# Both parts of x streamed as 512 columns in the feed-forward gate and up projections, and results rounded after the next job's first split, on one Trainium2 core

## What is computed

```
m = (jax.nn.sigmoid(z[..., o_gs:o_ga]) * (y_ssm @ w_proj_ssm[l])
     + jax.nn.sigmoid(z[..., o_ga:]) * (y_attn @ w_proj_attn[l]))
x = x + m @ w_out[l]
h = rms_norm(x, norm2_w[l], RMS_EPS)
x = x + (jax.nn.silu(h @ w_ffn_gate[l]) * (h @ w_ffn_up[l])) @ w_ffn_down[l]
```

## Time and profile before

| | |
|---|---|
| median of three runs | 2527.08 us |
| the profiled execution, its own time | 2526.77 us |
| its span, first to last instruction | 2525.0 us |
| TensorE busy | 2460.2 us, 97% |
| VectorE, ScalarE, GpSimd busy | 1475.3, 1129.0 and 186.0 us |
| granted TensorE clock, mean | 0.993 of full speed |

### The profile page before, as it was taken

The page is one execution under the profiler, slowest core; times in us unless marked ns, Lnnn a source line. Parts: engine busy times, 40 slices in busy tenths (PEclk is TensorE's granted clock), DMA queues, the critical chain, the costliest instruction groups (busy, mean ns, idle before and its releaser), DMA issues.

```text
span 2525.0 us, 45210 instructions
## 1 busy us (share of the span) xinstructions
PE 2460.2 (97%) x19625; PEld 2249.2 (89%) x19625; DVE 1475.3 (58%) x1814; ACT 1129.0 (45%) x1562; POOL 186.0 (7%) x198
## 2 busy tenths in 40 slices
PE   7999999999999999999999999999999999999997
PEld 7777888999889999999988899899888898999885
DVE  4899955565444545445444445745645567456555
ACT  5565555544444444444443344423544535234542
POOL 4000000001000000000000001310100051201000
PEclk9999999999999999999999999999999999999998
DMA  8444444454545555565555576423537664235465
GB/s 235 133 150 147 149 142 132 128 182 166 200 149 182 179 184 181 186 184 184 185 191 191 192 221 176 118 86 116 163 107 239 173 216 135 86 102 151 127 199 167
DMA packets 259414, 412.43 MB, mean 163 GB/s; under 512 B 53072, under 2 KB 74064, under 8 KB 258704
## 3 DMA queue, kind: packets, MB, share of 16 engines
q1 hardware_dynamic: 254496, 395.57, 50.7%
q0 software_dynamic: 4400, 13.89, 2.0%
q10 hardware_dynamic: 320, 0.08, 0.0%
HBM read 403.17 MB, written 6.30 MB: 162 GB/s over the span
## 4 chain that ended last, share of the span: by engine, by line
PE 90%; DVE 6%; ACT 2%; issue 1%; POOL 0%; DMA 0%; ACTq 0%; SPq 0%; DVEq 0%
PE bank L561 88%; DVE wp_lo L1069 2%; ACT wp_hi L1722 1%; PE bank L768 0%; DMA xt<-x 0%; DVE r_a L1548 0%; DVE rsd L1194 0%; DVE nsd L1461 0%; DVE r_kb L1550 0%; ACT L1722 0%; PE bank L662 0%; DVE xr L1715 0%; DVE xr L1713 0%; DVE sqr L1204 0%; POOL sgsA L2170 0%
## 5 line engine op out<-in xcount | busy, mean ns | idle before, releaser
L1069 DVE TENSOR_TENSOR wp_lo<-raw,wp_hi 128x1024 fp32r<-128x1024 f32 x740 | 921.0, 1251 | 893.9 <-ACT wp_hi L1722 893.5
L1722 ACT ACTIVATE wp_hi<-raw 128x1024 fp32r<-128x1024 f32 x740 | 782.5, 1060 | 1123.5 <-PE bank L561 1096.0
L561 PE MATMUL bank<-XX_hi,wp_hi 128*128 128x256 f32 x3840 | 1113.0, 290 | 10.8 <-DVE wp_lo L1069 9.7
L561 PE MATMUL bank<-XX_lo,wp_hi 128*128 128x256 f32 x3840 | 1087.5, 283 | 0.0
L561 PE MATMUL bank<-XX_hi,wp_lo 128*128 128x256 f32 x3840 | 1087.2, 283 | 0.0
L561 PEld LDWEIGHTS bank<-XX_hi,wp_hi 128*128 128x128 f32 x3840 | 736.6, 192 | 29.5 <-DVE wp_lo L1069 12.6
L561 PEld LDWEIGHTS bank<-XX_lo,wp_hi 128*128 128x128 f32 x3840 | 737.1, 192 | 2.2 <-issue 1.9
L561 PEld LDWEIGHTS bank<-XX_hi,wp_lo 128*128 128x128 f32 x3840 | 736.5, 192 | 0.0
L561 PE MATMUL bank<-wp_hi,FF_hi 128*128 128x512 f32 x352 | 137.3, 390 | 0.0
L561 PE MATMUL bank<-wp_hi,FF_lo 128*128 128x512 f32 x352 | 137.1, 389 | 0.0
L561 PE MATMUL bank<-wp_lo,FF_hi 128*128 128x512 f32 x352 | 137.1, 389 | 0.0
(11 more groups left out here) (476 smaller groups left out, 2774.7 us busy)
## 6 DMA issues: line engine op xcount, KB each, us to landing
raw<-w_in SPq DMA_DIRECT2D x304, 512.0 KB, 3.8
raw<-w_out SPq DMA_DIRECT2D x96, 512.0 KB, 4.1
raw<-w_ffn_gate SPq DMA_DIRECT2D x88, 512.0 KB, 3.8
raw<-w_ffn_up SPq DMA_DIRECT2D x88, 512.0 KB, 4.3
raw<-w_ffn_down SPq DMA_DIRECT2D x88, 512.0 KB, 3.6
raw<-w_proj_attn SPq DMA_DIRECT2D x16, 512.0 KB, 4.0
raw<-w_proj_ssm SPq DMA_DIRECT2D x16, 512.0 KB, 3.6
raw<-w_glu SPq DMA_DIRECT2D x8, 512.0 KB, 3.4
```

The source lines that it names most:

```text
L561: return e.matmul(o, lhsT, rhs, start=start, stop=stop, skip_group_check=True)
L1069: return tt(d, src, hi, SUB)
L1722: return e.activation(o, x, func, bias=bias, scale=scale)
```

## The change

1. `Pair` holds hi and lo in one buffer; `tiles(k)` gives both as a 128 x 2 x 256 view. For the 22 gate and up jobs (`wide`) a step has, per output tile, one matmul of w.hi with that view (512 columns, a whole bank: first half hi·hi, second half hi·lo) and one of w.lo with x.hi (256 columns, added to the first half). Each job takes four banks, 0 to 3 or 4 to 7.
2. The halves of a bank are added by VectorE with a `tensor_reduce` over a view that puts the halves innermost: four per job, 512 values in and 256 out per partition, into `gt` for gate and into `sqr` for up. ScalarE's SiLU now reads `gt` in SBUF and waits for these; up's multiply reads `gt` and `sqr`.
3. A function `rest` holds the rounding and subtraction of the results of `ps` and `fu`. Both engines call it after the split in the next job's first piece, not in `evac`.
4. VectorE's function `rest` for the mixer's angles is renamed; it does the same.

```
-        j.banks = (0, 1) if i % 2 == 0 else (2, 3)
+        j.banks = tuple(range(4 * (i % 2), 4 * (i % 2) + 4)) if j.wide else (0, 1) if i % 2 == 0 else (2, 3)
...
+    sides = lambda a: a.rearrange("p (h t) -> p t h", h=2)
...
+            elif j.wide:
+                for m in range(4):
+                    d, c = B[j.banks[m]], (512 * i + 128 * m, 512 * i + 128 * m + 128)
+                    mm(d, w.hi(*c), XX.tiles(k), first, False)
+                    last = mm(d[:, 0:256], w.lo(*c), XX.tile(k)[0], False, end)
...
 VectorE:
-                if n == "ps":
-                    e.wait_ge(*MSA("h", c))
-                    w = slice(1024 * c, 1024 * c + 1024)
-                    lo(MM.l[:, w], flat(sgs(c)), MM.hi_f(w.start, w.stop)).then_inc(MSV.made("l", c), 1)
...
+            elif n[:2] == "fg":
+                c = int(j.name[2:])
+                for m in range(4):
+                    if c > 1 and m % 2 == 0:
+                        e.wait_ge(*FSV("l", 2 * c - 4 + m // 2))
+                    w = slice(256 * (m % 2), 256 * (m % 2) + 256)
+                    e.tensor_reduce(gt[2 * (c % 2) + m // 2][:, w], sides(b[m]), AXX, ADD).then_inc(s_evV, 1)
             elif n[:2] == "fu":
...
-                e.wait_ge(s_evA, NA[f"fg{c}"])
+                for m in range(4):
+                    if c and m % 2 == 0:
+                        e.wait_ge(*FUV("m", 2 * c - 2 + m // 2))
+                    w = slice(256 * (m % 2), 256 * (m % 2) + 256)
+                    e.tensor_reduce(sqr[m // 2][:, w], sides(b[m]), AXX, ADD).then_inc(s_evV, 1)
                 for i in range(2):
-                    tt(g[i], g[i], b[i], MUL).then_inc(s_evV, 1)
-                for i in range(2):
-                    m = 2 * c + i
-                    e.wait_ge(*FSA("h", m))
-                    lo(FF.lo(512 * m, 512 * m + 512), g[i], FF.hi_f(512 * m, 512 * m + 512)).then_inc(FSV.made("l", m), 1)
+                    e.wait_ge(s_evV, j.freed[2 * i + 1][1])
+                    e.wait_ge(*FGA("s", 2 * c + i))
+                    tt(g[i], g[i], sqr[i], MUL).then_inc(FUV.made("m", 2 * c + i), 1)
...
+        def rest(name):
+            if name[:2] == "ps":
+                c = int(name[2:])
+                e.wait_ge(*MSA("h", c))
+                w = slice(1024 * c, 1024 * c + 1024)
+                lo(MM.l[:, w], flat(sgs(c)), MM.hi_f(w.start, w.stop)).then_inc(MSV.made("l", c), 1)
+            elif name[:2] == "fu":
+                c = int(name[2:])
+                for i in range(2):
+                    m = 2 * c + i
+                    e.wait_ge(*FSA("h", m))
+                    lo(FF.lo(512 * m, 512 * m + 512), gt[2 * (c % 2) + i], FF.hi_f(512 * m, 512 * m + 512)).then_inc(FSV.made("l", m), 1)
...
                         split(p + 3)
+                    if PIECE[p - 1][3]:
+                        rest(PIECE[p - 1][0].name)
                     if t + 1 == ENDS[j.name]:
                         evac(j)
...
 ScalarE (its rest and main change in the same way):
                 for i in range(2):
-                    if c > 1:
-                        e.wait_ge(*FSV("l", 2 * c - 4 + i))
-                    act(gt[2 * (c % 2) + i], b[i], ACT.Silu).then_inc(s_evA, 1)
...
+                    e.wait_ge(s_evV, j.freed[2 * i + 1][1])
+                    act(gt[2 * (c % 2) + i], gt[2 * (c % 2) + i], ACT.Silu).then_inc(FGA.made("s", 2 * c + i), 1)
```

More of the change, by code:

```diff
@@ L86, in __init__ @@
         self.name, self.W, self.pieces, self.KT = name, W, pieces, KT
-        self.home, self.tokens, self.first = home, tokens, first
+        self.home, self.tokens, self.first, self.wide = home, tokens, first, len(home) == 4
 class Pace:
@@ L178, in __init__ @@
         def __init__(self, name, n):
-            self.h, self.l = place(name + "_hi", n, F32R), place(name + "_lo", n, F32R)
+            self.both = v3(place(name + "_hl", 2 * n, F32R)[:, :], 2)
+            self.h, self.l = self.both[:, 0, :], self.both[:, 1, :]
         def hi(self, a, b):
@@ L194, in tile, with tiles @@
             return self.hi(256 * k, 256 * k + 256), self.lo(256 * k, 256 * k + 256)
+        def tiles(self, k):
+            return self.both[:, :, 256 * k:256 * k + 256]
     cst = alloc("cst", NCONST)
@@ L614, in step @@
             if first:
-                bank(j.banks[0], *freed(j.name, 0))
-                bank(j.banks[1], *freed(j.name, 1))
+                for m, b in enumerate(j.banks):
+                    bank(b, *freed(j.name, m))
             operand(j, k)
@@ L1078, in evac @@
             b = [B[x] for x in j.banks]
-            if n not in ("gs", "ga", "glu", "rg", "cg", "mg0", "mg1") and n[:2] != "fg":
+            if n not in ("gs", "ga", "glu", "rg", "cg", "mg0", "mg1"):
                 e.wait_ge(*over(j.name))
@@ L1348, in turn, with rest_of_angle @@
             last.then_inc(TU.made("fr", t), 1)
-        def rest(t):
+        def rest_of_angle(t):
             u = sets[t % 2]
@@ L1367, in _ @@
         turn(0)
-        rest(0)
+        rest_of_angle(0)
         for t in range(16):
@@ L1388, in _ @@
             if t < 15:
-                rest(t + 1)
+                rest_of_angle(t + 1)
             main(at.share(4.3))
@@ L1842, in evac, with rest @@
                     hi(MXc.hi(512 * i, 512 * i + 512), pair(cy, i)).then_inc(BXA.made("h", 2 * int(l) + i), 1)
+        def rest(name):
+            if name[:2] == "ps":
+                c = int(name[2:])
+                e.wait_ge(*GSP("a", 2 * c + 1))
+                hi(MM.hi(1024 * c, 1024 * c + 1024), flat(sgs(c))).then_inc(MSA.made("h", c), 1)
+            elif name[:2] == "fu":
+                c = int(name[2:])
+                for i in range(2):
+                    m = 2 * c + i
+                    e.wait_ge(*FUV("m", m))
+                    hi(FF.hi(512 * m, 512 * m + 512), gt[2 * (c % 2) + i]).then_inc(FSA.made("h", m), 1)
         def main(steps):
```

18 lines of the change are left out of this document (4 added, 14 removed).

## The result

The changed kernel takes 2511.45 us in the median of six runs (2508.51 to 2518.45), the kernel before 2527.18 (2525.52 to 2528.19); the ratio is 0.9944, 95% interval 0.9931 to 0.9957. It is faster, inside the range forecast and 0.75 us from the forecast. The six times lie in two places, though: 2508.5, 2508.7, 2510.8 and 2512.1, and 2518.1 and 2518.5. The kernel before keeps within 3 us. The profiled execution is the slowest of the six, with a span of 2516.7 us.

A forecast was written before the change was run, and what follows sets the result against it. TensorE, busy 97% of the span, was taken as the bound. Wide matmuls 18.8 + ps jobs 3.2 - fg2's end 2.7 - clock 2.9 = 16.4 us saved, from 2526.77 to 2510.4, median 2510.7; range 2506 to 2521.

The forecast's parts named there:

- The rate of the wide matmuls: Gate/up: a group takes 346.7 ns in place of 360.0, saving 13.3 ns in each of 1408 groups, 18.8 us.
- the sign named in the prediction: Gate/up trace: 512- and 256-column matmuls start 227 and 120 ns apart in turn, pieces 2.77 us apart.
- The 2.5 ns of the Trainium skill: Gate/up, opposing estimate: a removed instruction saves 2.5 ns, 3.5 us in all; result about 2526.
- The ps jobs: Ends of four ps jobs: rounding behind the next split gets back 0.80 us each, 3.2 us.
- The evacuations: End of fg: reduces 0.60 us apart, ScalarE's split 5.32 after its previous split's start (T), 0.38 to spare, cost 0.
- "Cost 0": End of fu: VectorE done at 7.11 us against 8.06 needed, 0.95 to spare; roundings follow the split, nothing lost.
- The end of fg2: Four reduces ahead of the angles delay everything by 2.40 us; TensorE late by 3.52, not 0.80: cost 2.72, idle 3.36.
- The clock: Behind fg2's idle time the granted clock drops, costing 2.9 us, bounds 0 and 3.2; no-drop rival: 2507.8, chance 0.28.
- the two that had a drop: Kernel before: idle times of 3.76 and 3.74 us, followed by granted clocks of 0.56 and 0.60.
- The sum: Whole kernel: 16.4 us saved, from 2526.77 to 2510.4, as a median of runs 2510.7; chance 0.40.
- dearer reduces: Rival, evacuations: outputs are paid for, 0.87 us per reduce, 9.5 us together, 2520.2; chance 0.11.

The follow-up runs named there:

- part 3 alone: Kernel before, with only rounding and subtraction of ps and fu results moved behind the next job's first split, no wide matmuls: 2524.04 us, ratio 0.9986.
- the wide-only kernel, grouped: Changed kernel with rounding and subtraction put back into the evacuation, and each step's four 512-column matmuls ahead of its four of 256: 2526.45 us.
- the grouped changed kernel: Changed kernel with each step's four 512-column matmuls ahead of its four of 256, nothing else changed: 2513.23 us.

## Why the prediction was right, and what it missed

**The rate of the wide matmuls** was right as a size and wrong as a constant. The 346.7 ns a group came from two streams of equal matmuls; at the quick pace it is 346.7. The sum held and its terms did not: the sign named in the prediction was starts of 227 and 120 ns in turn, and they are 231 or 232 and 115 or 116. A removed instruction saved 13 ns. The 2.5 ns of the Trainium skill, "TensorE: Matmul & The Clock Gate", section "Back-to-back issue gap", is for an isolated gap and isn't what it saves in this stream, as the trace of the kernel before had said. What the step took for granted, that a sequence of 512 and 256 columns has the sum of their rates, holds only in one of two paces. In the other a group takes 353.3, and 17 of 22 jobs then save 6.7 ns a group in place of 13.3: 7 us less of the 18.8.

**The ps jobs**: 3.2 forecast; by part 3 alone 3.0 between medians and 3.7 between profiles. The prediction took the loss to be 0.80 at each of the four; at ps3 it was 0.4 more.

**The evacuations**: reduces 0.60 apart as assumed, the split at T + 5.29 for 5.32, slack 0.32 for 0.38. At the end of fu ScalarE's split starts at T + 2.8, a piece later, and TensorE isn't late. "Cost 0" held.

**The end of fg2**: 2.40 us by four reduces forecast; from T to TensorE 9.18 before and 11.55 after, 2.37. The idle time printed is 3.32 for 3.36.

**The clock** fell in all three profiles of the changed kernel, at 2.9 us forecast and 2.8 measured. That my gap was nearer to the two that had a drop was a weak reason. Seven profiles have 3.2 to 3.3 us idle behind fg2; in six the clock fell, one of them at 3.23 us too (the wide-only kernel, grouped), and in the grouped changed kernel it didn't at 3.23. And the wait of 1.73 us in the attention stage was followed by a drop in two of the twelve profiles, and not in that of the kernel before.

**The sum** holds at the quick pace. Gate/up was to gain 18.8 - 2.7 - 2.9 = 13.2 us, and in the two profiles at that pace it is 13.0 and 12.9 us shorter; with 3.7 at ps the change gains 16.6 or 16.7, for 16.4 forecast. That is 2510.1, where half of the runs are (2508.5 to 2512.3); the others are 7 us and more above. My forecast describes the first set. That the median of six came within 0.75 us of it is luck: four of the six were quick, and the median of all 16 is 4 us above. The slower set lies inside the range only because that reached to 2521 for dearer reduces, which there were not. What remains open: why alternating 512 and 256 has two paces, and whether the 3 us of the attention stage's clock come with the change. Two of nine profiles of kernels with wide matmuls have that drop and none of three without, behind the same 1.73 us of idle time; that is too few to tell.

## What to carry to other kernels

Work out for each end of a job when the next operand is ready against when it is wanted, on each engine in its own order; here a rounding in front of a split cost some 10 us at the fu jobs, half of what 1408 saved matmuls gave, and 3.7 at the ps jobs. When an edit puts work into a place that is already late, move that place's other work first: spreading nine small instructions took away a wait, a drop of the clock and a restart that could cost the pace. And when the runs of a kernel fall into two sets, compare the distance of starts in a profile of each before looking for a cause in one.

## What the runs showed of the hardware

A TensorE stream that alternates 512 and 256 columns has two paces, 346.7 and 353.3 ns a group, drawn at a restart, after 0.3 us of delay as well as after 3 us, and kept as long as the engine isn't kept waiting; most of the difference, 5 ns, is in the 512-column matmul. Uniform streams ran at one pace each (120.0 and 226.7 ns). Four of one length followed by four of the other ran at 350.8 a group throughout one profile; in another at 350.8 up to a restart and 350.0 behind it.

A moving operand in two strips far apart streams as fast as one strip of 512 (2.77 us a piece in both, at the quick pace).

GpSimd's additions at ps now run beside VectorE's split, where VectorE waited before. The timelines at the end of ps0 with the change:

GpSimd:

```profile
588.58 3.53 POOL L2207 TENSOR_TENSOR sgsA<-sgsA,sga 128x512 f32<-128x512 f32 x2 [95.23 <-DVE sgsA L1118]
```

VectorE:

```profile
589.55 1.40 DVE L1081 TENSOR_TENSOR wp_hl<-raw,wp_hl 128x1024 fp32r<-128x1024 f32 x1 [0.46 <-ACT wp_hl L1755]
```


Two additions take 3.53 us where they took 2.55, and the split beside them 1.40 where others take 1.23. The second addition has all of the delay: it starts beside the split and takes 2.28 us in place of 1.29. It is so at all four ps jobs, and with part 3 alone as well. The slack at ps covered it; the 5.57 us from T to ScalarE's rounding became 6.56 (592.14 less 585.58).
